# A hybrid prompt-and-sample step: loads and splits moved across stage joints, sample rows stacked, first selected unit ahead of the compressed scores

## The reference

```
z = rmsnorm(x, norm1) @ w_in                      # 1024 -> 3608 columns
o_hg  = rmsnorm(gated linear scan(q, f, i)) * silu(g)    # 4 heads of 128
kc, vc = compress_rows(cached and new rows, cmp_w1, cmp_w2)   # blocks of 32 rows, stride 16
o_nsa = g0 * attend(q, kc, vc)                    # compressed blocks
      + g1 * attend(q, best 16 blocks of 64)      # selected ("SLC")
      + g2 * attend(q, last 512 tokens)           # window ("WND")
x = x + concat(o_hg, o_nsa) @ w_out
u = rmsnorm(x, norm2) @ w_gate;  v = rmsnorm(x, norm2) @ w_val
y = x + (gelu(conv3(u)) * v) @ w_down,  then a last norm
```

## Time and profile before

| what | us |
|---|---|
| median of 3 runs | 2449.77 |
| lowest, highest run | 2447.78, 2451.1 |
| the profiled execution's own time | 2453.46 |
| its span in the trace | 2451.7 |
| TensorE busy | 2282.1 (93%) |
| VectorE, ScalarE, GpSimd busy | 1306.6, 948.0, 514.1 |

### The profile page before, as it was taken

How to read it: one execution, slowest core, us unless ns; L and a number is a source line. 1 busy time by engine, 2 the same in 40 slices (tenths; PEclk the granted TensorE clock), 3 DMA queues, 4 the chain that set the end, 5 groups by cost and what they waited for, 6 DMA issues and landing times. The chain is left out here.

```text
span 2451.7 us, 40233 instructions
## 1 busy us (share of the span) xinstructions
PE 2282.1 (93%) x15950; PEld 2050.5 (84%) x15950; DVE 1306.6 (53%) x2960; ACT 948.0 (39%) x1911; POOL 514.1 (21%) x877
## 2 busy tenths in 40 slices
PE   6999989999999999859889896989999999999999
PEld 6999987777777877638767675869999999999998
DVE  5123028767767768633487785543333333355555
ACT  4124114554455544422275674212222222144444
POOL 0000004433334332200187683100000000011110
PEclk9999998999999999869799998999999999999999
DMA  4115627655446544098110002321111111122223
GB/s 118 68 52 185 231 85 233 221 184 172 160 158 197 184 152 123 26 261 276 35 61 5 9 7 96 129 67 43 43 51 43 43 51 43 51 81 80 79 70 117
DMA packets 213285, 263.10 MB, mean 107 GB/s; under 512 B 32386, under 2 KB 180098, under 8 KB 203746
## 3 DMA queue, kind: packets, MB, share of 16 engines
q1 hardware_dynamic: 194376, 157.61, 21.2%
q0 software_dynamic: 18752, 103.37, 12.2%
HBM read 202.76 MB, written 65.05 MB: 109 GB/s over the span
## 5 line engine op out<-in xcount | busy, mean ns | idle before, releaser
L1454 PE MATMUL f<-hH,wH 128*128 128x352 f32 x1056 | 341.4, 323 | 5.2 <-DVE wL L1340 5.2
L1454 PE MATMUL f<-hL,wH 128*128 128x352 f32 x1056 | 339.0, 321 | 0.0
L1454 PE MATMUL f<-hH,wL 128*128 128x352 f32 x1056 | 338.7, 321 | 0.0
L2407 ACT CAST a_XTH<-cpt 64x256 fp32r<-64x256 f32 (+1 forms) x576 | 201.1, 349 | 148.4 <-PE cpt L2614 137.8
L2524 DVE TENSOR_TENSOR a_XTL<-cpt,a_XTH 64x256 fp32r<-64x256 f32 (+1 forms) x576 | 230.3, 400 | 33.0 <-ACT a_XTH L2407 24.7
L1469 PE MATMUL f<-wdH,aH 128*128 128x256 f32 (+1 forms) x792 | 225.6, 285 | 4.1 <-DVE aL L1392 4.1
L1469 PE MATMUL f<-wdL,aH 128*128 128x256 f32 (+1 forms) x792 | 224.9, 284 | 0.0
L1469 PE MATMUL f<-wdH,aL 128*128 128x256 f32 (+1 forms) x792 | 224.9, 284 | 0.0
L2629 PE MATMUL cph<-a_XTH,a_w1H 128*128 128x512 f32 x512 | 217.5, 425 | 0.0
L2629 PE MATMUL cph<-a_XTH,a_w1L 128*128 128x512 f32 x512 | 205.8, 402 | 0.0
L2629 PE MATMUL cph<-a_XTL,a_w1H 128*128 128x512 f32 x512 | 204.9, 400 | 0.0
(11 more groups left out here) (464 smaller groups left out, 5445.4 us busy)
## 6 DMA issues: line engine op xcount, KB each, us to landing
v_s<-a_X SPq DMA_DIRECT2D x32, 512.0 KB, 6.3
raw<-in_w_in POOLq DMA_DIRECT2D x12, 1024.0 KB, 5.9
a_V<-v_s SPq DMA_DIRECT2D x6, 2048.0 KB, 14.8
raw<-in_w_gate SPq DMA_DIRECT2D x22, 512.0 KB, 3.8
raw<-in_w_val SPq DMA_DIRECT2D x22, 512.0 KB, 3.7
wraw<-in_w_down SPq DMA_DIRECT2D x44, 256.0 KB, 3.8
z_tok<-stage SPq DMA_DIRECT2D x48, 128.0 KB, 3.1
a_akq<-hq SPq DMA_DIRECT2D x32, 192.0 KB, 5.5
```

The lines of the kernel that those rows point to most:

```text
L1454: last = nc.tensor.matmul(bank[3 * a + n][:, 0:w], wp[:, a, k, :], hp[:, k, c0:c0 + w], start=(k + part == 0), stop=(k == KD - 1 and part ...
L2407: nc.scalar.copy(turned(XTH, u, s, k, g, a), split(bank(at, k)[:], u, k, g, a)).then_inc(h_ready, 1)
```

## The change

It has eight parts.

- The products of the sample tile in `project_in` (the groups without a gate), `project_out` and the down pass are stacked: the tile's high and low parts stand side by side as one stationary operand of 64 columns, so H*H and L*H come from one matmul in rows 0 to 31 and 32 to 63 of the bank, and VectorE adds the two halves.
- Tiles 0 and 1 of the cached rows are gathered inside `project_in`, in the place where `cmp_w1` was loaded; `cmp_w1` is loaded three groups later in four pieces of 1 MB, and six of its eight splits are made beside the last two groups.
- `compress_and_scan` begins with the turning of tile 0; the bias rows follow, the first chunk's scan products come after the first scores; `memset` of `XTH` and `XTL` covers only their last two columns; the prompt rows come in one buffer; from step 65 the first group's `s_x` is loaded into `room0`.
- `select` takes block maxima first, loads new rows, queries and two masks ahead on SyncE, and the gate product goes behind the first scores.
- The last 8 sample stores are issued in `prompt_attention`, behind the first four query loads.
- In each half of `prompt_attention` the unit SLC of tile 0 stands ahead of CMP, and the second head's keys are turned at step i = 1.
- The second half of `w_out`, and o and x of tiles 0 and 1, are loaded during `prompt_attention`; the scan's norm is made in `select`.
- In `project_out` o of tile 0 is split after one piece of `w_out`, and the products of tile 0 run over k outside and the two halves inside.

```diff
@@ project_in
+                if stacked(u):
+                    pe.wait_ge(xt_ready, 1)
+                    for k in range(KD):
+                        for wp, n in ((wH, 2 * DT), (wL, DT)) if k == 0 else ((wL, DT), (wH, 2 * DT)):
+                            last = nc.tensor.matmul(bank[u % 8][0:n, 0:nw], xt[:, k, 0:n], wp[:, j % 2, k, 0:nw],
+                                                    start=(k == 0 and wp is wH), stop=(k == KD - 1 and wp is wH))
...
                 if j == after_fm(2):
                     pool.wait_ge(qT_out, 16)
-                    pool.dma_start(keep["w1"][:].rearrange("p k q s h -> p (k q s) h"),
-                                   io["cmp_w1"][0].rearrange("k q (s u) d h -> (u d) (k q s) h", u=2)).then_inc(consts_sb["soft"]["p3_w1_in"], 16)
+                    pool.wait_ge(idx_step, 4)
+                    for i in range(2):
+                        for half in range(2):
+                            nc.gpsimd.indirect_dma_start(keep["X"][i][:, half].rearrange("p t n -> p (t n)"), None, cache,
+                                                         bass.IndirectOffsetOnAxis(ap=idx[:, half, i:i + 1], axis=0)).then_inc(x_in3[i], 16)
+                if j == after_fm(5):
+                    pool.wait_ge(hq_out, 16 * 3 * HH)
+                    for k in range(2):
+                        for q in range(2):
+                            pool.dma_start(keep["w1"][:, :, k, q], io["cmp_w1"][0, k, q].rearrange("(s u) d h -> (u d) s h", u=2)
                                           ).then_inc(consts_sb["soft"]["p3_w1_in"], 16)
@@ prompt_attention
-        for kind, qt in [(CMP, 0)] + [(kind, qt) for qt in range(NQ) for kind in (SLC, WND)]:
+        local = [(kind, qt) for qt in range(NQ) for kind in (SLC, WND)]
+        for kind, qt in local[:1] + [(CMP, 0)] + local[1:]:
...
+                if h == 1:
+                    for b in range(DB // 2):
+                        for g in range(NG):
...
+                if a == NQ:
+                    sp.wait_ge(s_ready, units[NU // 2].fill0)
+                    for k in range(4):
+                        sp.dma_start(keep["w5b"][:, k], io["w_out"][0, (4 + k) * P:(5 + k) * P, :]).then_inc(consts_sb["soft"]["p5_w_in1"], 16)
+                if a == NQ + 4:
+                    sp.wait_ge(qL_ready, R)
...
+                if i == 1:
+                    second_keys()
@@ project_out
+            high_of_w(0)
             high_of_o(0)
+            for k in range(1, KD):
+                high_of_w(k)
...
-                for h in range(2):
-                    if t >= 2:
+                for h, k in ([(h, k) for k in range(KD) for h in range(2)] if t == 0 else [(h, k) for h in range(2) for k in range(KD)]):
@@ feed_forward
+        def products(t, f):
+            r = rows_of(t)
+            if t < NT - 1:
+                return [(r, aH, wdH, f == 0, False), (r, aH, wdL, False, False), (r, aL, wdH, False, f == NF - 1)]
+            if f == 0:
+                return [(2 * r, aH, wdH, True, False), (r, aH, wdL, False, False)]
+            return [(r, aH, wdL, False, False), (2 * r, aH, wdH, False, f == NF - 1)]
@@ select
+            sp.dma_start(new_tok[:], z[T:TOK, 1280:1792]).then_inc(small_in, 16)
...
-            scores_in(0)
...
-            out(1)
...
+            block_maxima(0)
             dve.wait_ge(q_in, 32)
@@ compress_and_scan
+            for kind in range(2):
+                turn(0, kind)
             bias_rows()
-            for kind in range(3):
-                turn(0, kind)
+            turn(0, 2)
             bias_column()
```

More of the change, by code:

```diff
@@ L243, in _ @@
             sp.wait_ge(hq_out, 16 * 3 * HH)
+        cache = io["cache_nsa_kv"][0].rearrange("n (c t) s g d -> (n c) (t s g d)", t=4)
+        x_in3 = [consts_sb["soft"][f"p3_x_in{i}"] for i in range(2)]
         @block.gpsimd
@@ L898, in project_out @@
         soft = consts_sb["soft"]
[L899 removed]
+        w_in = [soft["p5_w_in0"], soft["p5_w_in1"]]
         wH_ready, wL_ready, oL_ready = sem("wH_ready"), sem("wL_ready"), sem("oL_ready")
@@ L1041, in keep_hT @@
                     last.then_inc(hT_kept, 1)
+            lows = Steps(dve, low_added)
+            rest_of_w(0)
             rest_of_o(0)
+            for k in range(1, KD):
+                rest_of_w(k)
+            dve.wait_ge(g2_in, 16)
             for t in range(NT):
@@ L1099, in _ @@
                 pe.wait_ge(oL_ready, 2 * t + 2)
-                for h in range(2):
-                    if t >= 2:
+                for h, k in ([(h, k) for k in range(KD) for h in range(2)] if t == 0 else [(h, k) for h in range(2) for k in range(KD)]):
+                    if t >= 2 and k == 0:
                         pe.wait_ge(x1_ready, 2 * (t - 2) + h + 1)
-                    for k in range(KD):
-                        if t == 0 and h == 0:
-                            pe.wait_ge(wL_ready, k + 1)
-                        for part, (op, wp) in enumerate(((oH, wH5), (oH, wL5), (oL, wH5))):
-                            last = nc.tensor.matmul(py[2 * (t % 2) + h][0:r, :], op[:, t % 2, k, 0:r], wp[:, k, 512 * h:512 * h + 512],
-                                                    start=(k + part == 0), stop=(k == KD - 1 and part == 2))
-                    last.then_inc(y_ready, 1)
+                    if t == 0 and h == 0:
+                        pe.wait_ge(wL_ready, k + 1)
+                    for rows, op, wp, first, final in products(t, k):
+                        last = nc.tensor.matmul(py[2 * (t % 2) + h][0:rows, :], op[:, t % 2, k, 0:rows], wp[:, k, 512 * h:512 * h + 512],
+                                                start=first, stop=final)
+                    if k == KD - 1:
+                        last.then_inc(y_ready, 1)
                 if t >= 1:
@@ L1467, in _ @@
                         pe.wait_ge(wdL_ready, NGR * c + f // 2 + 1)
-                    for part, (ap, wp) in enumerate(((aH, wdH), (aH, wdL), (aL, wdH))):
-                        last = nc.tensor.matmul(bank[t % 3][0:r, 0:QW], ap[:, h, j, 0:r], wp[:, f, :],
-                                                start=(f + part == 0), stop=(f == NF - 1 and part == 2))
+                    for rows, ap, wp, first, final in products(t, f):
+                        last = nc.tensor.matmul(bank[t % 3][0:rows, 0:QW], ap[:, h, j, 0:rows], wp[:, f, :], start=first, stop=final)
                     if f == NF - 1:
@@ L2013, in _ @@
             last.then_inc(kn_ready, 1)
-            pe.wait_ge(sig_ready, 1)
-            pe.wait_ge(mask_in, 96)
-            for G in range(2):
-                last = nc.tensor.matmul(misc[:, 448 + 24 * G:472 + 24 * G], rowtok[:, G, :], gates[:], start=True, stop=True)
-            last.then_inc(g_ready, 1)
             pe.wait_ge(q_ready, 1)
@@ L2021, in _ @@
             small_scores(0)
-            pe.wait_ge(g_kept, 1)
+            pe.wait_ge(sig_ready, 1)
+            pe.wait_ge(mask_in, 64)
+            for G in range(2):
+                last = nc.tensor.matmul(po[:, 448 + 24 * G:472 + 24 * G], rowtok[:, G, :], gates[:], start=True, stop=True)
+            last.then_inc(g_ready, 1)
             choose(0)
@@ L2551, in _ @@
             dve.wait_ge(q_ready, 1)
-            dve.wait_ge(xt_clear, 1)
-            for k in range(2):
-                low_parts(0, k)
+            low_parts(0, 1)
             keys(0)
@@ L2835, in hybrid_step @@
             with ExitStack() as later:
-                keep["w1"] = later.enter_context(nc.sbuf_tensor("w1", W1_SHAPE, F32))
+                with ExitStack() as raw:
+                    keep["room0"] = raw.enter_context(nc.sbuf_tensor("room0", [P, PAST + DS], F32))
+                keep["X"] = [later.enter_context(nc.sbuf_tensor(f"X{i}", [P, 2, 4, 512], F32)) for i in range(2)]
+                later.enter_context(nc.sbuf_tensor("behind_X", [P, 16], F32))
+                with ExitStack() as raw:
+                    keep["w1"] = raw.enter_context(nc.sbuf_tensor("w1", W1_SHAPE, F32))
+                keep["w1L"], keep["w1H"] = (later.enter_context(nc.sbuf_tensor(n, W1_SHAPE, F32R)) for n in ("w1L", "w1H"))
             with ExitStack() as low:
@@ L2883, in hybrid_step @@
             keep["hH"] = at(high, "hH", [P, KD, TOK], F32R)
-            with ExitStack() as front:
-                keep["w5b"] = at(front, "w5b", [P, 4, D])
             keep["hL"] = at(high, "hL", [P, KD, TOK], F32R)
```

358 lines of the change are left out of this document (225 added, 133 removed).

## The result

| | before | changed |
|---|---|---|
| median, us | 2450.43 (4 runs) | 2414.97 (4 runs) |
| lowest to highest | 2447.78 to 2451.67 | 2412.41 to 2418.52 |
| the profiled execution's span | 2451.7 | 2410.6 |

The account below looks back on a forecast made before the run. TensorE, busy 2282.1 of 2451.7 us, was taken as the bound, so gains come from fewer matmuls or its 169.6 us idle. Terms 16.6 + 9.5 + 8.2 + 5.0 + 6 + 10.5 = 55.8 gave 2394, range 2386 to 2402.

Parts of the forecast that it names:

- Stacked sample rows: Sample tile in `project_in`, `project_out` and the down pass: one of three matmuls goes, gaining 4.3, 2.8 and 9.5, 16.6 us in all.
- 0.6 for the three other passes, whose bank comes free one addition later: Down pass: 0.6 us taken off the 10.5 us stacking gain, because three passes get their bank one addition later.
- Start of the scan's stage: Start of `compress_and_scan`: six of eight `w1` splits move into `project_in`, gaining 9.5 us, bounds 6 and 12.
- Six eighths are 10.2: Scan's start: the `w1` split took 13.5 us, six eighths of it are 10.2, less 0.7 for the turns standing first.
- Start of `select`: Start of `select`: earlier loads, `s_x` already there and maxima moved ahead gain 8.2 us, bounds 0 and 11.
- The sample stores: Between `select` and the attention: eight store issues move behind four query loads, gaining 5.0 us, bounds 3 and 5.
- Start of the attention: Attention: SLC of tile 0 first and key turns at step 1 gain 6 us with the second half, bounds 0 and 10.
- Rival B: Part is given back: attention 0, `select` 4, `project_out` 6, scan's start 6; gain 37.6, total 2412 us; chance 0.15.
- Start of `project_out`: Start of `project_out`: early loads, the norm made ahead and products following piece by piece gain 10.5 us, bounds 6 and 13.
- The prediction's own sign of failing: Whole kernel: the forecast fails if TensorE's idle time, 169.6 us, stays over 140 or its busy time falls under 10.
- Rival D: `project_in`: `cmp_w1` lands late and TensorE stops; slower, 2451 us at a lag of 84 us, 2467 at 100; chance 0.02.

## Why the prediction was wrong

- *Stacked sample rows.* The mechanism was right everywhere and the loads stayed hidden. In the input stage 4.7 came (4.3). In the down pass the bare saving was 10.5, as forecast (by 0.120 a matmul, which rows 3 have from a tile of 128 rows; the sample tile's took 0.113 to 0.118), and the step that failed is "0.6 for the three other passes, whose bank comes free one addition later". The bank was not what came late: the refill of `aH` and `aL` and the next weights was. The joints and the addition kept 6.7 of the 10.5, where 1.0 was allowed. I had read 160 us of VectorE's time in 292 as slack.
- *Start of the scan's stage.* 9.3 measured, 9.5 forecast, but the step behind it was wrong. "Six eighths are 10.2" took the splits as the whole chain, while the 64 bias matmuls run beside them: the early splits are worth 4.8 to 5.9, the smaller memsets, which I had not counted, 3.5. The first such product came 8.0 us sooner, not 9.5. The sum came right by two errors of opposite sign.
- *Start of `select`.* 8.1 for 8.2. The first turn of `room` came at 1056.83, 26.3 us after TensorE's last work of the scan, against 34.0 before. The maxima start at 1033.77, before the first scores, with no wait for `s_x`; the wait of 7.12 for the key blocks is what remains of the start:

```profile
1033.77 4.40 DVE L1859 TENSOR_REDUCE a_bm<-room 128x64 f32<-128x4096 f32 x1
...
1042.72 1.03 PE L2045 MATMUL r_sc<-a_kvc,a_qblk 128*32 128x256 f32 x2 [7.12 <-DMA a_kvc<-kvc]
...
1056.83 1.54 PE L2080 MATMUL r_tr<-ident,room 128*128 128x128 f32 x6 [3.75 <-ACT room L1802]
```

- *The sample stores.* 5.6 at the joint for 5.0; at like clock 0.8 of it was given back in the attention, within the scatter.
- *Start of the attention.* This is the step that decided. "Now SLC of tile 0 comes first and the turns stand at step 1, where scores run ahead. Gain 6": from its first matmul on the attention took 309.1 us instead of 304.3, a loss of 4.8 at the same mean clock of 0.91, and TensorE's idle time in its first 60 us grew from 9.5 to 14.3, where under 4 was forecast. I counted TensorE's idle time as something that a new order would fill, and did not work out what each engine has at hand at the moment. With CMP first, ScalarE's and VectorE's work on the compressed part lies beside TensorE's longest stretch of scores. With SLC first the same work lies between the first probabilities and their product, and TensorE has run out of scores. Rival B had this place with 0 and no loss; my bounds (0 to 10) should have gone below nothing. B's total, 2412, came nearest to the measured one, but by parts that did not happen: it gave 4 us to `select` and 6 to the scan's start, where 8.1 and 9.3 came.
- *Start of `project_out`.* 14.8 for 13.3 with the sample tile: its wait of 16.9 became 6.24, and tile 0's products ended 22.9 us after the attention's last, against 34.3.
- *Sum and range.* With the two failed terms as measured (-4.8 and 3.8 in place of 6 and 9.5) the sum is 39.3 and the profiled execution 2414, where it had 2412.4. Both terms erred the same way, and the attention's lower end was set above what the engines beside TensorE had to do. Against 2394 the median missed by 6.3 more than the traces' 14.7: I took off 3.7 for the trace's distance from the median, and the changed kernel's trace lay 2.6 on the other side. The prediction's own sign of failing held: TensorE's idle time stayed at 148.6, over the 140 named. Rival D's two times were added up wrongly: by its own terms a lag of 84 us gives 2394 + 84 - 22.5 = 2455.5, and 100 us 2471.5; nothing hangs on them, since `project_in` became 4.7 us shorter, with no stop for the load.

## What to carry to other kernels

When matmuls are taken out of a tile, look at what the other engines do in the time of that one tile, not in the stage: here it was the stretch where weights and the next tile are split, 87% full where the stage's average is 55%. When units are put in another order, write down for every engine what it has ready at each step; filling one engine's idle time with work that the others must first serve makes a new wait. And undo each part of a change alone even where the sum is right: two terms here, the starts of the scan and of `select`, were right as sums while their parts were not. And before one trace's stage length is set against another's, set their granted clocks beside it: one list of the attention took 300.9 at 0.92 and 305.0 at 0.91.

## What the runs showed that I had not expected

- A product of 128x4 on VectorE took 2.47 us beside GpSimd's 3.62 us product over SBUF, and 0.16 to 0.37 otherwise.
- Matmuls of 256 columns with 32 or 64 stationary columns follow each other in 0.113 to 0.118 us in the down product, those with 128 in 0.120.
- The same code's scan took 674.3 to 684.1 us from trace to trace, and the longest had 2.1 us more of idle time than the changed kernel's 677.4, and a clock of 0.96 against 0.97; what lowers the clock stays open.
- With one and the same list of units the attention took 306.8 to 316.0 us, as the clock where its second head starts was 0.94 to 0.80.
